# Pairs written out, the convolution one pair ahead, and the order of the projection groups in a hybrid attention and convolution block

## What is computed

```python
hn = _rmsnorm(h, mix_norm_g[i])
proj = jnp.einsum('bld,dc->blc', hn, w_in[i])
q, k, v, ca, cg = jnp.split(proj, [SB_WIDTH, 2 * SB_WIDTH, 3 * SB_WIDTH, 3 * SB_WIDTH + CONV_CHANNELS], axis=-1)
# attention, by head: z = q.k / sqrt(64), keys before the query only
rev = lax.cumsum(log_1m_beta, axis=3, reverse=True)
excl = jnp.concatenate([rev[..., 1:], jnp.zeros_like(rev[..., :1])], axis=-1)
w = jnp.where(mask, jnp.exp(log_beta + excl), 0.0)
# convolution: u = ca * sigmoid(cg), 31 taps over time, bias, layer norm, silu
mixed = jnp.concatenate([attn, conv], axis=-1)
h = h + jnp.einsum('blc,cd->bld', mixed, w_out[i])
h = h + jnp.einsum('blf,fd->bld', jax.nn.silu(g) * u, w_down[i])
```

## Time and profile before

| | us |
|---|---|
| median of 3 runs | 1293.19 (1290.79 to 1293.56) |
| profiled execution | 1292.85 |
| its span, first to last instruction | 1291.1 |
| TensorE busy in it | 1205.9 (93%) |
| VectorE busy | 743.9 (58%) |
| GpSimd busy | 490.4 (38%) |
| ScalarE busy | 457.8 (35%) |

### The profile page before, as it was taken

How to read it: one execution, slowest core, us unless ns; L and a number is a source line. 1 busy time by engine, 2 the same in 40 slices (tenths; PEclk the granted TensorE clock), 3 DMA queues, 4 the chain that set the end, 5 groups by cost and what they waited for, 6 DMA issues and landing times.

```text
span 1291.1 us, 16227 instructions
## 1 busy us (share of the span) xinstructions
PE 1205.9 (93%) x6108; PEld 1010.0 (78%) x6108; DVE 743.9 (58%) x781; ACT 457.8 (35%) x881; POOL 490.4 (38%) x374
## 2 busy tenths in 40 slices
PE   5999999999988868998899999999999999999996
PEld 4798878878877657886678778787878787878775
DVE  4327997997995994558644343433433434343446
ACT  4312462462462752444431322223131323141323
POOL 5212201201100141124582737465564747382921
PEclk9999999999998879999999999999999999999999
DMA  5304102102002401111212111212111212111113
GB/s 191 123 25 108 34 18 66 32 16 66 16 0 50 180 17 33 33 49 38 77 34 66 33 65 33 66 33 65 36 65 64 65 33 65 52 47 66 33 33 146
DMA packets 55554, 73.44 MB, mean 57 GB/s; under 512 B 1732, under 2 KB 45828, under 8 KB 55238
## 3 DMA queue, kind: packets, MB, share of 16 engines
q1 hardware_dynamic: 54310, 70.49, 17.4%
q10 hardware_dynamic: 1184, 2.13, 0.4%
HBM read 62.03 MB, written 6.32 MB: 53 GB/s over the span
## 4 chain that ended last, share of the span: by engine, by line
PE 57%; DVE 16%; POOL 12%; issue 9%; ACT 3%; DMA 2%; DVEq 0%; POOLq 0%; SPq 0%; ACTq 0%
PE ps L1597 18%; PE ps L1576 16%; PE ps L1407 13%; DVE gq L1114 7%; PE ps L1525 4%; POOL wa_lo L586 4%; PE ps L1365 4%; DVE acc L1071 3%; POOL wb_lo L586 2%; DVE wbeta L1119 2%; POOL wa_f L623 1%; POOL wa_f L617 1%; POOL wa_f L620 1%; PE ps L1465 1%; DMA out<-ost 1%
## 5 line engine op out<-in xcount | busy, mean ns | idle before, releaser
L1288 DVE TENSOR_TENSOR mix<-ps,mix 128x512 f32<-128x512 f32 x176 | 121.3, 691 | 137.5 <-PE ps L1597 137.5
L1071 DVE SCALAR_TENSOR_TENSOR acc<-u_pad,parp,acc 128x1024 f32<-128x1024 f32 x116 | 157.3, 1400 | 0.2
L1597 PE MATMUL ps<-wd_hi,act_hi 128*128 128x512 f32 x352 | 137.0, 389 | 1.5 <-DVE act_lo L1277 1.5
L523 POOL TENSOR_TENSOR wp_lo<-raw,wp_hi 128x1024 fp32r<-128x1024 f32 x16 | 45.2, 2825 | 243.6 <-ACT wp_hi L686 179.1
L1597 PE MATMUL ps<-wd_hi,act_lo 128*128 128x512 f32 x352 | 136.9, 389 | 0.0
L1597 PE MATMUL ps<-wd_lo,act_hi 128*128 128x512 f32 x352 | 136.9, 389 | 0.0
L586 POOL TENSOR_TENSOR wa_lo<-wa_f,wa_hi 128x512 fp32r<-128x512 f32 x58 | 79.1, 1366 | 138.7 <-ACT wa_hi L893 134.7
L1407 PE MATMUL ps<-hn_hi,wp_hi 128*128 128x348 f32 (+2 forms) x352 | 119.8, 340 | 2.3 <-DVE par L1086 2.3
L1407 PE MATMUL ps<-hn_lo,wp_hi 128*128 128x348 f32 (+2 forms) x352 | 118.8, 337 | 0.0
L1407 PE MATMUL ps<-hn_hi,wp_lo 128*128 128x348 f32 (+2 forms) x352 | 118.5, 337 | 0.0
L1114 DVE TENSOR_TENSOR_SCAN gq<-gq,ones 128x1040 f32<-128x1040 f32 (+4 forms) x64 | 105.3, 1645 | 9.8 <-ACT wbeta L805 9.5
(11 more groups left out here) (162 smaller groups left out, 2747.4 us busy)
## 6 DMA issues: line engine op xcount, KB each, us to landing
raw<-in_w_gate SPq DMA_DIRECT2D x11, 1024.0 KB, 5.4
raw<-in_w_up SPq DMA_DIRECT2D x11, 1024.0 KB, 5.3
wd_f<-in_w_down SPq DMA_DIRECT2D x11, 1024.0 KB, 4.8
raw<-in_w_in SPq DMA_DIRECT2D x20, 512.0 KB, 3.8
kd<-kd SPq DMA_DIRECT2D x4, 1040.0 KB, 6.8
xin<-in_x SPq DMA_DIRECT2D x8, 512.0 KB, 3.6
wo_raw<-in_w_out SPq DMA_DIRECT2D x4, 1024.0 KB, 8.1
mix<-in_x SPq DMA_DIRECT2D x8, 512.0 KB, 3.3
```

Source lines behind the costliest of these rows:

```text
L523: pool.tensor_tensor(dst, raw[:, slot, :], hi.bitcast(F32), ALU.subtract).then_inc(wlo_done, 1)
L1071: dve.scalar_tensor_tensor(out=acc[:, j % 2, :], in0=u_pad[:, j:j + L], scalar=parp[:, j:j + 1], in1=acc[:, j % 2, :], op0=ALU.mult, op1=A ...
L1288: dve.tensor_tensor(hrow, ps[:, TB + n % 4, :], hrow, ALU.add).then_inc(d_added, 1)
L1597: last = pe.matmul(ps[:, TB + n % 4, :], a[s][:, t, i * P:(i + 1) * P], w_[m][:, t, dh * BANK:(dh + 1) * BANK], start=(t == 0 and s == m = ...
```

## The change

- **Pairs written out.** No loop is left; the functions `pair`, `groups` and `tap` take the pair as a plain number, and one list, `PROJ`, holds all groups of the program in order, from which every semaphore count is taken.
- **Convolution a pair ahead.** `cg` and `ca` of the next pair come first in a pair, before its `k` and `q`. The sigmoid and the gate product write straight into one of two input buffers, `u_pad[:, p % 2]`, and taps read their weights from `par`; `u_next`, `parp` and `conv_input` are gone. 24 steps of the first pair's convolution stand ahead of the pairs. In each pair VectorE ends the pair's own convolution before `k` and does eighteen steps of the next: nine between the key and query groups, two behind the first two units and seven behind units 9 to 15.
- **Order of k and q.** `k` 0, `k` 1, `q` 0, `k` 2, and `q` 1 between the scores of units 1 and 2. The two first groups of a pair are computed in the tail of the pair before it.
- **Key copy in two transfers**, of 696 columns after `k` 1 and of 344 after `k` 2; unit 4 is the first whose scores wait for the second.
- **w_out's low parts** are computed by VectorE, four behind units 12 to 15 of the last pair and four behind the first normalise step.
- In a pair's opening one score and two transposes change places, and ScalarE copies the first two transposes before the sigmoids of unit 4.

```diff
-    GROUPS = ([("k", g) for g in range(3)] + [("q", g) for g in range(2)]
-              + [("cg", g) for g in range(3)] + [("ca", g) for g in range(3)])
+    GROUPS = ([("cg", g) for g in range(3)] + [("ca", g) for g in range(3)]
+              + [("k", 0), ("k", 1), ("q", 0), ("k", 2), ("q", 1)])
+
+    def groups_of(p):
+        ahead = [(kind, g, p + 1) for kind, g in GROUPS[:6]] if p + 1 < PAIRS else []
+        return ahead + [(kind, g, p) for kind, g in GROUPS[6:]]
+
+    PROJ = [(kind, g, 0) for kind, g in GROUPS[:6]] + [t for p in range(PAIRS) for t in groups_of(p)]
...
+            def copy_keys(p, g, cols):
+                sp.wait_ge(*freed("k", g, p))
+                sp.dma_start(kd[DH:2 * DH, :, :, cols].bitcast(F32), kd[0:DH, :, :, cols].bitcast(F32)).then_inc(k_dup[g - 1], 16)
+
+            def pair_loads(p):
+                more = p + 1 < PAIRS
                 if more:
-                    load_tile(CH_LOOP + 4 * p, 0, w_in_t, CG0 + P * (p + 1))
-                    load_tile(CH_LOOP + 4 * p + 1, 1, w_in_t, CA0 + P * (p + 1))
+                    for kind, q in WEIGHTS[4 + 4 * p:6 + 4 * p]:
+                        load_weight(kind, q)
+                else:
+                    copy_keys(p, 1, slice(0, 2 * W3))
                 sp.wait_ge(pv_used, past(NT * p))
...
+                if more:
+                    for kind, q in WEIGHTS[6 + 4 * p:8 + 4 * p]:
+                        load_weight(kind, q)
+                if more:
+                    copy_keys(p, 1, slice(0, 2 * W3))
+                copy_keys(p, 2, slice(2 * W3, T))
...
             def pair(p, more):
-                for g in range(3):
-                    split_hi("k", g, p)
                 if more:
-                    hi(CH_LOOP + 4 * p, 0, wp(0), used_up("k", p))
+                    sigmoid_gate(p + 1, range(2 if p else 0, 3))
+                    hi_weight("k", p, used_up("cg", p + 1))
+                    hi_weight("q", p, used_up("ca", p + 1))
+                    for g in range(2):
+                        split_hi("k", g, p)
                 split_hi("q", 0, p)
+                split_hi("k", 2, p)
                 if more:
+                    hi_weight(*WEIGHTS[6 + 4 * p], used_up("k", p))
...
+            taps = [list(range(CONV_K + 1)) for _ in range(PAIRS)]
+            some_taps(0, taps[0], 24)
+
+            def w_out_lo(k):
+                dve.wait_ge(wo_hi_s, k + 1)
+                dve.tensor_tensor(wo_lo[:, k, :], wo_raw[:, k, :], wo_hi[:, k, :].bitcast(F32),
+                                  ALU.subtract).then_inc(wo_lo_s, 1)
...
+                now, ahead = taps[p], taps[p + 1] if more else None
+                if more:
+                    some_taps(p, now, len(now) - 8)
+                    for g, n in zip(range(3), (3, 3, 2)):
+                        glu(g, p + 1)
+                        some_taps(p, now, n)
+                    assert not now
+                    for (kind, g), n in zip(GROUPS[6:10], (2, 3, 2, 2)):
                         split_lo(kind, g, p)
+                        some_taps(p + 1, ahead, n)
+                else:
+                    for (kind, g), n in zip(GROUPS[8:10], (2, 1)):
+                        split_lo(kind, g, p)
+                        some_taps(p, now, n)
...
-                    if n < 2 and not more:
-                        some_taps(p, rest, 2 + n)
-                    if n == 1:
-                        evac(*groups[-1])
-                    elif more and n > 7:
-                        some_taps(p + 1, early, 1)
+                    if n == HELD_BACK - 1:
+                        split_lo("q", 1, p)
+                    if more and (n < 2 or n > 8):
+                        some_taps(p + 1, ahead, 1)
                     elif not more:
-                        some_taps(p, rest, 1)
+                        some_taps(p, now, 1)
+                    if not more and n >= WO_AT + 6:
+                        w_out_lo(n - WO_AT - 6)
...
+            for p in range(PAIRS - 1):
+                pair(p, {NU - 1: lambda: groups(groups_of(p + 1)[:1]), NU: lambda: groups(groups_of(p + 1)[1:2])})
```

More of the change, by code:

```diff
@@ L845, in pair @@
                         act.activation(wo_hi[:, k, :], wo_raw[:, k, :], ACT.Copy).then_inc(wo_hi_s, 1)
-                if not more:
+                if p + 2 < PAIRS:
+                    sigmoid_gate(p + 2, range(2))
+                elif more:
+                    for g in range(2):
+                        split_hi("k", g, p + 1)
+                else:
                     mix_hi(1, 0)
                 evac_attention(1, NU - 1)
-            with act.Fori(0, PAIRS - 1) as p:
-                pair(p, True)
-            pair(PAIRS - 1, False)
+            for p in range(PAIRS):
+                pair(p, p + 1 < PAIRS)
             def ln_silu_of(i):
```

277 lines of the change are left out of this document (125 added, 152 removed).

## The result

| | us |
|---|---|
| before, median of 4 runs beside it | 1293.38 (1290.79 to 1295.03) |
| after, median of 4 runs | 1273.47 (1272.63 to 1275.82) |
| ratio | 0.9851, 95% interval 0.9829 to 0.9873 |
| profiled execution of after | 1272.63, span 1270.9 |

The change makes the kernel 1.5% faster. The forecast was 1276, with a range of 1262 to 1289.

What follows compares the result with a forecast made beforehand. VectorE's chain of scans was taken to end last, with TensorE 93% busy. Third pair's end +6.4 us, then the last pair's shorter stretches, made -16.6 in all: 1292.85 - 16.6 = 1276 us, range 1262 to 1289.

Steps and rivals of the forecast that it cites:

- R to S, looped pairs: From the last unit's transpose (R) to the next pair's first score (S) on TensorE: falls from 45.8 to 44.0 us.
- TensorE's own work between S and R: First score to last unit's transpose, looped pairs: 44.5 plus 1.8, 46.3 us, as a large group replaces a small one.
- rival A: TensorE is full: VectorE keeps pace and every pair takes what TensorE needs, giving 1244 us; chance 0.04.
- VectorE's chain: Looped pairs, first score to last unit's transpose: scans, products, low parts and ten taps sum to 53.6 us, before 50.0.
- GpSimd's cost: Two GpSimd subtractions per looped pair between first score and last transpose still slow VectorE, about 4.1 us, unchanged.
- rival B: TensorE's waits grow and its clock halves, 2 us per fall: 1288, or 1293 if more; 0.07 for over 1289.
- The looped pairs: Each looped pair takes 44.0 + 53.6 = 97.6 us in place of 95.8, 1.8 longer than before.
- First pair: First score at 144.8, 0.8 us earlier, including 1 us waiting for the last gate product; last-unit transpose 2.8 later.
- Last pair: Third pair's last transpose to first score 21.1 us (was 26.3), then to last transpose 55.8 (was 73.6), 17.8 less.
- D: Last pair's long scans come from weight traffic, not GpSimd, so it does not shorten as said: 1292 us; chance 0.04.
- C: Key copy stands behind weight loads on SyncE's queue, so TensorE waits at the first score: at worst 1308; chance 0.05.
- The sum: Whole program: third pair's last transpose 6.4 us later, last pair's at 470.5 against 487.11, so -16.6 us in all.

Runs made afterwards that it cites:

- short_sub: Changed kernel with GpSimd's two looped-pair subtractions between first score and last-unit transpose cut to 64 of 1024 columns (result incomplete): 1261.70 us, ratio 0.9746.
- taps_two: Changed kernel without taps behind units 9 to 15 in the first two pairs; they follow the last unit's transposes: 1276.05 us, ratio 0.9854.
- late_sub: Changed kernel, looped pairs' taps behind units 9-15 removed, 13 last-pair taps in third pair's tail, ScalarE's high parts behind units 8 and 11: 1254.09 us.
- wout_gpsimd: Changed kernel with w_out's eight low parts back on GpSimd in the last pair: 1290.27 us, ratio 0.9974 to the kernel before.
- wout_alone: Kernel before the change, with only w_out's eight low parts moved to VectorE: 1279.14 us, ratio 0.9890.
- one_copy: Changed kernel with the second half of the keys filled by one transfer behind k's third group instead of two: 1311.15 us, ratio 1.0133.
- late_only: Changed kernel with only ScalarE's two high parts, and so GpSimd's subtractions, moved behind units 8 and 11; taps stay: 1276.22 us, ratio 0.9856.

## Why the prediction was right

**R to S, looped pairs (44.0): right**, 44.01. **TensorE's own work between S and R (46.3): right**, 46.2 to 46.4 at a full clock in four of the kernels above. **As the length that the stretch would fall to without VectorE it was wrong**, and with it the sentence that VectorE ends last because its sum is over 46.3, and rival A's 1244: TensorE waits 3.3 us for the opening and for ScalarE's copies in the change's order even without the meetings (short_sub), and 4.8 with them, at a lower clock (taps_two). The bound was 52.8 and not 46.3; without VectorE's taps a pair would have gained 0.6 to 0.9 us, not 7. The forecast didn't suffer from this only because VectorE's 53.6 is still the higher of the two. That it is higher, by under 1 us, was luck: nothing in the prediction secured it.

**VectorE's chain (53.6): right**, 54.03, 53.66 and 54.27, its 52.7 busy being the sum's terms. **GpSimd's cost (4.1, unchanged): right in size, wrong in place.** I let the first subtraction meet the taps behind `k` 2. The taps were ahead of it; GpSimd waited for them (its span is 5.08) and then met unit 0's product. On VectorE that costs the same: 2.0 us on this product, and 2.0 on the one that meets the second subtraction (3.21 instead of 1.24); the prediction had a row for the first meeting alone. On TensorE it made the opening late: waits of 0.70, 1.84 and 0.81 us lie between 147.8 and 152.7 in the first pair, and behind them the granted clock is 0.50 from 152.5 to 155.5:

```profile
152.50:155.50 3.00, 2.80 (x10) 2.37 (x10) 2.73 (x6) 1.81 (x7) 0.00 (x0) 0.50 0.00 0
```

In short_sub and late_sub, where the opening's waits are 0.75 and 0.81 us, the clock is 1.00 in all three pairs. The fall is rival B's mechanism at a small scale; its price of 2 us per fall was taken where TensorE is the later engine, and here VectorE's chain covered it. **The looped pairs (+1.8 each)** came to +1.9 and +2.5.

**First pair: right but for the stall.** Its groups took 39.75, the forecast 39.8, and the 1 us of wait for the last gate product did not come: there is no wait on TensorE ahead of S. **The idle VectorE before the gate product** is there, 11 us as said:

```profile
214.65 0.52 DVE L1048 TENSOR_TENSOR u_pad<-ps,u_pad 128x348 f32<-128x348 f32 x1 [11.36 <-PE ps L1420]
```

**Last pair: right**, R(2) to S 21.19 (forecast 21.1, in which 0.2 had no row; without the wait for the keys the stretch had been 21.36), S to R 55.86 (55.8), together -22.9 (forecast -23.0). wout_gpsimd and wout_alone size the first of its causes, 13.2 to 14.7 us. What is left of 17.8, 3 to 5 us, goes to the other two, fewer taps and no late query group; I did not part them. D and C were wrong: no scan is long there, and no key wait shows, though one_copy measured what C was afraid of (8.8 us a pair, 38 in all, against my 32 for three pairs).

The Trainium skill's rule for the port ("SBUF — State Buffer", section "Who interferes with whom") would have all of a meeting lost. The first meeting of the second pair cost VectorE 2.02 us (2.46 against 0.44), with 2.40 for a subtraction that meets nothing, and the two together 4.0 by short_sub. The rule's mechanism agrees with the trace. By its 4.8 for two meetings S to R would have been 54.3, by my 4.1 53.6; the three pairs lie from 53.66 to 54.27 and don't tell the two apart.

**The sum.** -16.6 forecast. By the marks, without the lead-in, -16.3 up to the last R. The 2.9 us of clock in the lead-in and 1.0 in the rest of the program, neither forecast, make the profiled execution's 20.2. I didn't test the 1.0: the other kernels show 803.6 to 805.2 for that part, the kernel before 804.0.

## What to carry to other kernels

"What this engine has to do" is a lower bound of a stretch that begins with an empty pipeline, but no forecast of it: add the waits of its opening and those for any third engine, and read them in the list of waits by stretch before pricing work moved off the other engine. Where two chains are within 1 us of each other, an edit to either shows next to nothing (taps_two, late_only), and only the pair of edits shows what each is worth. A subtraction of 2.4 us on GpSimd cost VectorE about 2.0 us of it in each meeting with a scan or a product here; move it to a stretch with slack on VectorE, or to VectorE itself, where w_out's took 1.22 us each and no operation beside them was long.

## What the runs showed of the hardware

The wait between the two engines goes both ways. In short_sub GpSimd's subtraction of 64 columns took 3.01 us in each looped pair where it came behind VectorE's two taps, and 0.40 at the other place:

```profile
240.00 3.01 POOL L571 TENSOR_TENSOR wp_lo<-raw,wp_hi 128x64 fp32r<-128x64 f32 x1 [14.49 <-ACT wp_hi L693]
254.45 0.40 POOL L571 TENSOR_TENSOR wp_lo<-raw,wp_hi 128x64 fp32r<-128x64 f32 x1 [11.44 <-ACT wp_hi L693]
```

VectorE's taps and scan ended at 242.89 there, 0.12 ahead of GpSimd's end, so it found no place between the taps. These are the rows of VectorE:

```profile
239.79 2.47 DVE L1085 SCALAR_TENSOR_TENSOR acc<-u_pad,par,acc 128x1024 f32<-128x1024 f32 x2
242.18 0.71 DVE L1137 TENSOR_TENSOR_SCAN gq<-gq,ones 128x272 f32<-128x272 f32 x1
```

With the scans and products that a subtraction made longer (4.22 instead of 2.05 us, 2.46 instead of 0.44), scans, products and taps all take part.

The clock does not fall each time that the waits look alike. late_only's three looped pairs are built alike; each has waits of up to 2.2 us for VectorE near its end, all are 53.62 long, and the clock was 1.00, 0.97 and 1.00 in them. The fall in the second lies in its last 9.4 us, where the mean is 0.82, and cost no time, since VectorE is the later engine there.
